# Expert rows gathered in four 256-column pieces and turned by VectorE block transposes; gate and up weights in contiguous rows; up in two halves

## The chip, the cores and the metric

The kernel runs on one core of one Trainium2 chip. The metric is the device time of one execution in microseconds (us), as the median of several runs; lower is better. Everything is float32. Five engines have a queue of their own each: TensorE (PE in the profile; PEld is its weight load), VectorE (DVE), ScalarE (ACT), GpSimd (POOL) and SyncE (SP). Each runs its instructions in the order in which they stand, and they meet at semaphores.

## The reference

One layer of an encoder, applied to a prompt of 2048 tokens and 8 x 16 sample tokens: 17 tiles of 128 tokens of width 1024. The change touches the query weights of the attention and the experts:

```python
def memory_attend(h, mem_k, mem_v, w_xq, w_xo):
    B, T, _ = h.shape
    q = (h @ w_xq).reshape(B, T, X_HEADS, X_HEAD_DIM)
    s = jnp.einsum('bqhd,bkhd->bhqk', q, mem_k.astype(q.dtype)).astype(jnp.float32) * (X_HEAD_DIM ** -0.5)
    p = jax.nn.softmax(s, axis=-1).astype(q.dtype)
    o = jnp.einsum('bhqk,bkhd->bqhd', p, mem_v.astype(q.dtype)).reshape(B, T, D_MODEL)
    return o @ w_xo

def routed_experts(t, expert, w_eg, w_eu, w_ed):
    # t: (n, 1024); expert: (n, 2), the two experts of 32 that each token takes; assignments sorted by expert
    ...
    def expert_block(args):
        xb, e = args
        return (jax.nn.silu(xb @ w_eg[e]) * (xb @ w_eu[e])) @ w_ed[e]
    ...

def trunk_layer(...):
    h = rms_norm(x, g_mix)
    z = h @ w_in
    ...
    x = x + jnp.concatenate([a_out, b_out], axis=-1) @ w_out
    x = x + memory_attend(rms_norm(x, g_xattn), mem_k, mem_v, w_xq, w_xo)
    x = x + hier_moe(rms_norm(x, g_ffn), w_rg, b_rg, w_re, b_re, w_eg, w_eu, w_ed)
    return x, new_hist, v
```

An expert has gate and up matrices of 1024 x 512 and a down matrix of 512 x 1024. `hier_moe` picks a group of 4, two experts of 8 in it, calls `routed_experts` and adds its two rows per token by their gates.

## The kernel before

The stages follow one another: mixing (17 tiles, to about 852 us), a fold of `w_xq` and `w_xo` into two matrices A and B, the sample attention, a stage of attention and router (17 tiles, to about 1530 us), and the expert stage (to the end).

**Token rows and their turn.** A product needs the features on the partitions. In the attention stage `turn_split` (L217) turns a tile of 128 x 1024 by one DVE block transpose; it leaves the features in another order than a PE transpose does, and `w_xq`, from which A is made, is loaded in four DMAs so as to match that order (L399).

**The experts.** The router stores for each expert a list of rows (token, place, gate) in `table_scratch`. An expert step works on 128 rows in two lanes of 64: lane 0 with one expert, lane 1 with another, each expert's weights in its part of W (a part holds gate, up and down, 4096 columns each). `both` (in PE's part) issues a pass for both lanes: 64 rows of lane 0 and 64 rows of lane 1 on the two halves of the array, each against 512 columns of its own expert. There are 42 steps: one for tile 0 that is mixed into the end of the attention stage, and 41 by `work`, called from `expert_steps` (L1416): three in a row, a loop of 12 passes over two steps, an inner loop of 5 passes over two steps, and four in a row.

**A step on PE** (`work`, L2176): gate in 8 calls of `both` into `psg`; up in 8 into `psu`; then the transposes of the next tile's rows (`turn_x`, into `pst`, 8) woven with those of the hidden rows (`turn_h`, 4); down in 16 passes into `psx`. ACT makes silu of the gate (L1746), copies the lower half of the turned hidden rows (L1751) and the lower half of the turned token rows (L1756). DVE multiplies silu by up in two halves (`hidden`, L1937), copies the upper halves (L1942, L1929), adds the result into the rows of the token (`add_x`, L1956) and scales the output (L1962, L1965). `hidden` waits for the whole of up.

**A step on POOL** (order of `work`, L1645): `gather_x` (L1580, the rows that the result is added to), `gather(t+2)` (L1572, the rows that go in, one indirect DMA of 128 rows of 4 KB), `fetch(t+3)` (L1556, two DMAs of 64 list rows, one per lane), `fetch_again(t+1)` (the same for the list that the scatter uses), `scatter_x` (L1586), a small power (L1593) and `scatter_out` (L1599). `gather_x` waits until the scatter of the tile before has landed. All of these transfers go through the software queue q0; the weights go through q1, issued by SP (`load_part`, L1274), which loads the next expert's gate, up or down matrix as soon as PE is done with the part that it replaces, in rows of 512 columns (2 KB) for gate and up and of 1024 columns (4 KB) for down.

**Between the router and the experts** the last router tile scatters its lists (L1551), then POOL fetches the lists of tile 1 and gathers its rows, PE turns them and the first step of the loop begins. The names in the traces are those of the memory: `r_pss` holds `psg` and `psu`, `r_psx` is `psx`, `r_psr` and `r_psk` are the two halves of the turned hidden rows, `r_x1n` the gathered rows, `r_h2T` the turned ones, `r_x1r` the hidden rows, `e_pair` and `e_spair` the two fetched lists.

## Time and profile before

| | us |
|---|---|
| median of 3 runs | 2493.62 (2493.59 to 2493.75) |
| profiled execution | 2493.03 |
| its span | 2491.4 |
| granted TensorE clock over the span | 0.991 |
| PE busy | 2421.9 (97%) |
| DVE busy | 942.2 (38%) |
| POOL busy | 559.3 (22%) |
| ACT busy | 470.4 (19%) |

A share of 97% says that PE is the engine to look at, but not whether a microsecond less of its work is a microsecond less of time: that is read from the waits of each stage. In the profile's 40 slices the DMA engines are the busiest in the expert stage, at 0.4 to 0.9 of the time, and nearly idle before it.

### The profile page before, as it was taken

Reading aid. Unit: us, or ns where it says so; the run is one execution under the profiler, and the core shown is the slowest. Engines: PE = TensorE matmul, PEld = TensorE weight load, DVE = VectorE, ACT = ScalarE, POOL = GpSimd, SP = SyncE. Lnnn points to the kernel's source line nnn. Section 1 sums busy time; section 2 is a strip of 40 time slices with the busy share of each in tenths; the row PEclk is TensorE's granted clock in tenths of the full one; section 3 lists DMA queues with packets and bytes.
Section 4 is the critical chain, followed back from the end, with each engine's and each line's share of the span. In section 5 each row is a group of like instructions: output and inputs, shape, how many; then the busy total and the mean of one; then the engine's idle time right before and its main releaser. Section 6 shows DMA issues by size and latency. Waiting matters only on the chain.

```text
span 2491.4 us, 29996 instructions
## 1 busy us (share of the span) xinstructions
PE 2421.9 (97%) x9375; PEld 1104.5 (44%) x9376; DVE 942.2 (38%) x2519; ACT 470.4 (19%) x1042; POOL 559.3 (22%) x711
## 2 busy tenths in 40 slices
PE   8999999999999997999999998999999999999998
PEld 4444444444444574455555553333333333333332
DVE  1586756747676102233333334122212222222222
ACT  2222222222111122222222221111111111111111
POOL 1122132222213100011111112232333322323231
PEclk9999999999999998999999999999999999999999
DMA  6211111011153516522222117967497749797994
GB/s 234 106 40 56 39 64 39 34 64 38 41 189 78 185 42 245 177 65 64 68 68 68 59 52 270 326 227 266 158 362 258 260 161 367 256 348 266 347 348 147
DMA packets 168279, 403.67 MB, mean 162 GB/s; under 512 B 25650, under 2 KB 34370, under 8 KB 168178
## 3 DMA queue, kind: packets, MB, share of 16 engines
q1 hardware_dynamic: 137314, 327.81, 37.9%
q0 software_dynamic: 30656, 74.14, 8.1%
q8 instruction: 51, 0.84, 0.1%
q10 hardware_dynamic: 216, 0.54, 0.1%
q14 instruction: 42, 0.34, 0.0%
HBM read 336.15 MB, written 80.66 MB: 167 GB/s over the span
## 4 chain that ended last, share of the span: by engine, by line
PE 58%; DMA 1%; issue 1%; DVE 0%; POOL 0%; ACT 0%; POOLq 0%; ACTq 0%; DVEq 0%
PE r_pss L2162 22%; PE r_psx L2162 11%; PE r_psx L2124 9%; PE r_pss L2105 9%; PE r_pst L2151 2%; PE r_psr L2133 1%; PE r_psr L2173 1%; PE r_pst L2116 1%; PE r_pss L2163 1%; PE r_pst L2097 1%; PE r_psk L2173 0%; PE r_psx L2163 0%; DMA table_scratch<-r_val,r_slot 0%; PE r_pss L2210 0%; DMA r_x1n<-h_scratch,e_token 0%
## 5 line engine op out<-in xcount | busy, mean ns | idle before, releaser
L2162 PE MATMUL r_pss<-W,r_h2T 128*64 x1312 | 572.3, 594 | 3.3 <-issue 3.3
L2163 PE MATMUL r_pss<-W,r_h2T 128*64 128x512 f32 x1312 | 572.4, 594 | 0.0
L788 PE MATMUL a_psz<-W 128*128 128x512 f32 x1088 | 479.4, 594 | 0.1
L626 DVE SCALAR_TENSOR_TENSOR yacc<-aext,pcol,yacc 128x256 f32<-128x256 f32 x928 | 370.8, 476 | 0.0
L2162 PEld LDWEIGHTS r_pss<-W,r_h2T 128*64 128x64 f32 x1312 | 180.1, 137 | 373.6 <-issue 373.6
L788 PEld LDWEIGHTS a_psz<-W 128*128 128x128 f32 x1088 | 203.0, 191 | 235.2 <-issue 234.7
L2162 PE MATMUL r_psx<-W,r_x1r 128*64 x656 | 290.1, 595 | 2.3 <-ACT r_x1r L1751 0.2
L2163 PE MATMUL r_psx<-W,r_x1r 128*64 128x512 f32 x656 | 290.3, 595 | 0.0
L2124 PE MATMUL r_psx<-W 128*128 128x512 f32 x544 | 236.5, 592 | 1.2 <-ACT W L1696 1.2
L2105 PE MATMUL r_pss<-W,r_h2T 128*128 128x512 f32 x512 | 224.4, 596 | 2.3 <-PEq L123 2.3
L2163 PEld LDWEIGHTS r_pss<-W,r_h2T 128*64 128x64 f32 x1312 | 180.2, 137 | 0.0
L491 POOL TENSOR_TENSOR W<-W 128x512 f32<-128x512 f32 x34 | 115.6, 3409 | 268.5 <-ACT W L603 268.5
L1937 DVE TENSOR_TENSOR r_x1r<-r_pss,r_x1r 128x256 f32<-128x256 f32 x84 | 31.7, 418 | 368.9 <-PE r_pss L2163 338.6
L2162 PEld LDWEIGHTS r_psx<-W,r_x1r 128*64 128x64 f32 x656 | 86.5, 137 | 172.8 <-issue 172.8
L2124 PEld LDWEIGHTS r_psx<-W 128*128 128x128 f32 x544 | 102.0, 190 | 123.4 <-issue 123.4
L2105 PEld LDWEIGHTS r_pss<-W,r_h2T 128*128 128x128 f32 x512 | 96.5, 191 | 117.9 <-issue 117.9
L1956 DVE SCALAR_TENSOR_TENSOR r_x<-r_psx,e_spair,r_x 128x512 f32<-128x512 f32 x84 | 63.0, 750 | 226.8 <-PE r_psx L2163 226.8
L955 PE MATMUL a_psz<-W,a_maT 128*128 128x512 f32 x272 | 122.3, 592 | 0.0
L955 PE MATMUL a_psz<-W 128*128 128x512 f32 x272 | 122.3, 592 | 0.0
L1586 POOL DMA_INDIRECT x_scratch<-r_x,e_stoken x41 | 42.6, 1039 | 343.6 <-DVE r_x L1956 322.7
L1776 ACT ACTIVATE r_x1r<-r_x 128x512 f32<-128x512 f32 x84 | 52.9, 630 | 288.6 <-DVE r_x L1956 288.5
L1551 POOL DMA_INDIRECT table_scratch<-r_val,r_slot x34 | 34.8, 1023 | 255.9 <-DVE r_slot L1909 250.8
(351 smaller groups left out, 2374.1 us busy)
## 6 DMA issues: line engine op xcount, KB each, us to landing
W<-in_w_expert_gate SPq DMA_DIRECT2D x32, 2048.0 KB, 11.6
W<-in_w_expert_up SPq DMA_DIRECT2D x32, 2048.0 KB
W<-in_w_expert_down SPq DMA_DIRECT2D x32, 2048.0 KB
W<-in_x_prompt SPq DMA_DIRECT2D x32, 512.0 KB, 4.2
...
```

Of the source, the lines that this page charges most:

```text
L491: pool.tensor_tensor(x, mixed[:, 512 * n:512 * n + 512], x, ALU.add).then_inc(S["x1_half"], 1)
L626: ins = dve.scalar_tensor_tensor(out=out, in0=src, scalar=w, in1=yacc[:, i, :], op0=ALU.mult, op1=ALU.add)
L788: last = pe.matmul(psz[bank][:], hT[t.par][:, k, :], w_in[bank][:, k, :], start=(k == 0), stop=(k == KD - 1))
L955: last = pe.matmul(psz[n][:], (maT[:, k, :] if k < CG else mbl[t.par][:, k - CG, :]), w_out[:, k, 512 * n:512 * n + 512], start=(k == 0), ...
L1586: pool.indirect_dma_start(out=x2_d.rearrange("t p d -> (t p) d"), out_offset=bass.IndirectOffsetOnAxis(ap=stoken[t.par][:], axis=0), in_=y ...
L1776: act.activation(junk_f, yb[t.par][:, 512 * m:512 * m + 512], ACT.Square, scale=1 / 32, accum_out=fss[:, t.par, m:m + 1]).then_inc(F["squa ...
L1956: dve.scalar_tensor_tensor(out=yb[t.par][:, c], in0=psx[:, c], scalar=spair[t.par][:, 1:2], in1=yb[t.par][:, c], op0=ALU.mult, op1=ALU.add ...
L2105: last = pe.matmul(pss[:, 2 * n:2 * n + 2, :].rearrange("p h n -> p (h n)"), h2T[i % 2][:, k, :], A[:, k, 512 * n:512 * n + 512], start=(k ...
L2124: last = pe.matmul(psx[:, 512 * n:512 * n + 512], (pT if i else qT)[:, c, :], (B if i else w_xo)[:, c, 512 * n:512 * n + 512], start=(c == ...
L2151: last = pe.transpose(pst[:, k, :], xg[t.par][:, P * k:P * k + P], ident[:])
L2162: pe.matmul(out[0:HALF, :], xt[:, 0:HALF], W[:, bass.ds(base + at, 512)], start=start, stop=stop)
L2163: return pe.matmul(out[HALF:P, :], xt[:, HALF:P], W[:, at:at + 512], start=start, stop=stop)
```

## The change

1. `turn_split` reads its source at a stride of 8 elements, which gives the feature order 8p + k on partition p. `w_xq` is loaded in that order in one DMA, and the norm's gains (`gx`) by a small DMA of its own.
2. Gate and up matrices are loaded as 8 consecutive rows per partition (16 KB in one piece). Down is as before.
3. The rows of an expert tile are gathered by four indirect DMAs of 128 x 256 columns (1 KB per row), each with its own column of indices 4 x token + quad. The index columns come from four fetches of 128 x 3 in place of two of 64 x 3. One DVE `turn_split` turns the tile; PE's `turn_x` and the copies on ACT and DVE are gone, also for tile 0, whose transposes stood in the scores of the last token tile.
4. Up is computed in two halves of 256 columns, the first into `psu`, the second into `psk`, and `hidden` half 0 waits for the first only. Both halves of the hidden rows are turned right behind up.

```diff
         def turn_split(dve, dst, src):
 
-            return dve.transpose(dst.rearrange("p k (b r) -> p b k r", r=QUAD), src.rearrange("p (b k a) -> p b k a", b=QUADS, a=QUAD))
+            return dve.transpose(dst.rearrange("p k (b r) -> p b k r", r=QUAD), src.rearrange("p (b a k) -> p b k a", b=QUADS, a=QUAD))
...
-                            for q in range(QUADS):
-                                sp.dma_start(w_xq[QUAD * q:QUAD * q + QUAD, :, :],
-                                             I["w_xq"][0][D // QUADS * q:D // QUADS * q + D // QUADS, :].rearrange("(k a) n -> a k n", a=QUAD)).then_inc(wxq_here, 16)
+                            sp.dma_start(w_xq, I["w_xq"][0].rearrange("(p k) n -> p k n", p=P)).then_inc(wxq_here, 16)
...
+                    act.dma_start(gx[:], I["g_xattn"][0].rearrange("(p k) -> p k", p=P)).then_inc(gx_here, 16)
...
-                                                  scale=gcol[:, KD + k:KD + k + 1])
+                                                  scale=gx[:, k:k + 1])
...
-                          I[name][0][bass.ds(e, 1), :, :].rearrange("a (k p) n -> p (a k) n", p=P)).then_inc(here, 16)
+                          I[name][0][bass.ds(e, 1), :, :].rearrange("a (k p) n -> p (a k) n" if n == 2 else "a (p k) n -> p (a k) n", p=P)).then_inc(here, 16)
...
-            psh = [psr[:].rearrange("p (j n) -> p j n", j=4), psp]
+            psh = psr[:].rearrange("p (j n) -> p j n", j=4)
+            psh_hi = psu[:, 256:512].rearrange("p (j n) -> p j n", j=2)
+            ups = [psu[:, 0:256], psk[:, 0:256]]
...
+                    def fetch_quad(par, lane, h, rows):
+
+                        pool.dma_start(pair[par][:, 2 * lane + h, :], rows.unsqueeze(0).to_broadcast([QUADS, QUAD, 3])).then_inc(pair_here[par], 16)
+
                     def fetch(t):
                         need(pool, T["token_done"], t.v - 1)
                         settle(pool)
-                        fetch_pairs(t, pair[t.par], pair_here[t.par])
+                        for lane in range(LANES):
+                            base = pool.value_load(steps_row[0:1, lane, bass.ds(t.v, 1)], min_val=0, max_val=NE * REG - HALF)
+                            for h in range(2):
+                                fetch_quad(t.par, lane, h, table_d[bass.ds(base + QUAD * h, QUAD), :])
 
                     def fetch_again(t):
...
                     def gather(t):
                         pool.wait_ge(T["token_done"], t.v + 1)
-                        need(pool, T["x_turned"], 2 * (t.v - 1))
+                        need(pool, T["xT_done"], t.v - 1)
                         settle(pool)
-                        pool.indirect_dma_start(out=xg[t.par][:], out_offset=None,
-                                                in_=h3_d[0:P * (EARLY + 2), :] if isinstance(t.v, int) and t.v == 0 else h3_d,
-                                                in_offset=bass.IndirectOffsetOnAxis(ap=token[t.par][:], axis=0)).then_inc(x_here[t.par], 16)
+                        h3_rows = h3_d[0:P * (EARLY + 2), :] if isinstance(t.v, int) and t.v == 0 else h3_d
+                        for b in range(QUADS):
+                            c = D // QUADS
+                            pool.indirect_dma_start(out=xg[t.par][:, c * b:c * b + c], out_offset=None,
+                                                    in_=h3_rows.rearrange("t (q c) -> (t q) c", q=QUADS),
+                                                    in_offset=bass.IndirectOffsetOnAxis(ap=token[t.par][:, b:b + 1], axis=0)).then_inc(x_here[t.par], 16)
...
                     def tokens(t):
-                        dve.wait_ge(pair_here[t.par], 32 * (t.half + 1))
-                        need(dve, x_here[t.par], 16 * t.half)
-                        dve.tensor_copy(token[t.par][:], pair[t.par][:, 0:1]).then_inc(T["token_done"], 1)
+                        dve.wait_ge(pair_here[t.par], 16 * QUADS * (t.half + 1))
+                        need(dve, x_here[t.par], 16 * QUADS * t.half)
+                        dve.tensor_scalar(token[t.par][:], pair[t.par][:, :, 0], float(QUADS), quad[:], ALU.mult, ALU.add).then_inc(T["token_done"], 1)
 
                     def xT_out(t):
-                        dve.wait_ge(T["x_turned"], 2 * t.v + 2)
+                        dve.wait_ge(x_here[t.par], 16 * QUADS * (t.half + 1))
                         need(dve, T["up_done"], t.v)
-                        dve.tensor_copy(xT[t.par][:, 4:8, :], pst[:, 4:8, :]).then_inc(T["xT_done"], 1)
+                        turn_split(dve, xT[t.par][:], xg[t.par][:]).then_inc(T["xT_done"], 1)
 
                     def hidden(t):
                         dve.wait_ge(T["silu_done"], t.v + 1)
-                        dve.wait_ge(T["up_done"], t.v + 2)
                         need(dve, T["h_turned"], 2 * t.v)
                         for m in range(2):
+                            if m == 0 and not (isinstance(t.v, int) and t.v == 0):
+                                dve.wait_ge(T["up_half"], t.v)
+                            else:
+                                dve.wait_ge(T["up_done"], t.v + 2)
                             c = slice(256 * m, 256 * m + 256)
-                            dve.tensor_tensor(hb[:, c], psu[:, c], sg[:, c], ALU.mult).then_inc(T["h_done"], 1)
+                            up = psu[:, c] if isinstance(t.v, int) and t.v == 0 else ups[m]
+                            dve.tensor_tensor(hb[:, c], up, sg[:, c], ALU.mult).then_inc(T["h_done"], 1)
 
                     def hT_out(t):
                         dve.wait_ge(T["h_turned"], 2 * t.v + 2)
                         dve.wait_ge(T["down_done"], t.v + 1)
-                        dve.tensor_copy(hT[:, 2:4, :], psh[1][:, 0:2, :]).then_inc(T["hT_hi"], 1)
+                        dve.tensor_copy(hT[:, 2:4, :], psh_hi).then_inc(T["hT_hi"], 1)
...
-                    def turn_x(t, ks):
-                        if ks[0] == 0:
-                            pe.wait_ge(x_here[t.par], 16 * (t.half + 1))
-                            need(pe, T["xT_done"], 2 * t.v)
-                        for k in ks:
-                            last = pe.transpose(pst[:, k, :], xg[t.par][:, P * k:P * k + P], ident[:])
-                        if ks[-1] in (3, 7):
-                            last.then_inc(T["x_turned"], 1)
-
                     def weights(t):
                         e = pe.value_load(steps_row[0:1, 2, bass.ds(t.v, 1)], min_val=0, max_val=EPL - 1)
                         wanted = pe.value_load(steps_row[0:1, 3, bass.ds(t.v, 1)], min_val=16, max_val=16 * NE)
                         return pe.value_load(slot_base[0:1, bass.ds(e, 1)], min_val=EXPERT_COLS, max_val=2 * EXPERT_COLS), wanted
 
-                    def both(out, xt, base, at, start, stop):
-
-                        pe.matmul(out[0:HALF, :], xt[:, 0:HALF], W[:, bass.ds(base + at, 512)], start=start, stop=stop)
-                        return pe.matmul(out[HALF:P, :], xt[:, HALF:P], W[:, at:at + 512], start=start, stop=stop)
+                    def both(out, xt, base, at, start, stop, n=512):
+
+                        pe.matmul(out[0:HALF, :], xt[:, 0:HALF], W[:, bass.ds(base + at, n)], start=start, stop=stop)
+                        return pe.matmul(out[HALF:P, :], xt[:, HALF:P], W[:, at:at + n], start=start, stop=stop)
 
                     def turn_h(t, m):
                         pe.wait_ge(T["h_done"], 2 * t.v + m + 1)
-                        if m and isinstance(t.v, int) and t.v == 1:
-                            pe.wait_ge(T["loads_known"], 1)
                         if m == 0:
                             need(pe, T["hT_lo"], t.v)
                             need(pe, T["hT_hi"], t.v)
                         for k in (2 * m, 2 * m + 1):
-                            last = pe.transpose(psh[m][:, k - 2 * m, :], hb[:, P * k:P * k + P], ident[:])
+                            last = pe.transpose(psh_hi[:, k - 2, :] if m else psh[:, k, :], hb[:, P * k:P * k + P], ident[:])
                         last.then_inc(T["h_turned"], 1)
 
                     def work(t, j=-LAST):
                         base, wanted = second if isinstance(t.v, int) and t.v == 1 else weights(t)
                         pe.wait_ge(gate_here, wanted)
-                        pe.wait_ge(T["xT_done"], 2 * t.v + 2)
+                        pe.wait_ge(T["xT_done"], t.v + 1)
                         need(pe, T["silu_done"], t.v)
                         for k in range(KD):
                             last = both(psg, xT[t.par][:, k, :], base, 512 * k, k == 0, k == KD - 1)
                         last.then_inc(T["gate_done"], 1)
                         pe.wait_ge(up_here, wanted)
                         need(pe, T["h_done"], 2 * t.v)
-                        for k in range(KD):
-                            last = both(psu, xT[t.par][:, k, :], base, 4096 + 512 * k, k == 0, k == KD - 1)
-                        last.then_inc(T["up_done"], 1)
-                        more = j < LAST - 1
-                        if more:
-                            turn_x(t.at(1), (0, 1, 2, 3))
+                        for m in range(2):
+                            if m and isinstance(t.v, int) and t.v == 1:
+                                pe.wait_ge(T["loads_known"], 1)
+                            for k in range(KD):
+                                last = both(ups[m], xT[t.par][:, k, :], base, 4096 + 512 * k + 256 * m, k == 0, k == KD - 1, 256)
+                            last.then_inc(T["up_done" if m else "up_half"], 1)
                         turn_h(t, 0)
-                        if more:
-                            turn_x(t.at(1), (4, 5))
                         turn_h(t, 1)
-                        if more:
-                            turn_x(t.at(1), (6, 7))
                         pe.wait_ge(down_here, wanted)
...
                             scores(s, 0)
-                            if s + 1 == NT:
-                                pe.wait_ge(S["pT_done"], NT - 2)
-                                turn_x(fixed(0), (0, 1, 2, 3))
-                                turn_x(fixed(0), (4, 5, 6, 7))
                             scores(s, 1)
...
-                    turn_x(fixed(1), (0, 1, 2, 3))
-                    turn_x(fixed(1), (4, 5, 6, 7))
```

In the body of the first expert loop on PE, between the end of up and the first down pass, stood before (`r_pst` the turned token rows):

```order
L2163 MATMUL r_pss<-W,r_h2T 64x512
L2148 ISA
L88 ISA
L2151 MATMUL r_pst<-ident,r_x1n 128x128 x4
L2166 REGISTER_ALU
L2173 MATMUL r_psr<-ident,r_x1r 128x128 x2
L2151 MATMUL r_pst<-ident,r_x1n 128x128 x2
L2173 MATMUL r_psk<-ident,r_x1r 128x128 x2
L2151 MATMUL r_pst<-ident,r_x1n 128x128 x2
L2162 ISA
L2162 MATMUL r_psx<-W,r_x1r 64x512
```

and stands now, with two 256-column passes of up's second half ahead:

```order
L2161 MATMUL r_psk<-W,r_h2T 64x256
L2162 MATMUL r_psk<-W,r_h2T 64x256
L2161 ISA
L2161 MATMUL r_psk<-W,r_h2T 64x256
L2162 MATMUL r_psk<-W,r_h2T 64x256
L2165 REGISTER_ALU
L2170 MATMUL r_psr<-ident,r_x1r 128x128 x2
L2165 REGISTER_ALU
L2170 MATMUL r_pss<-ident,r_x1r 128x128 x2
L2161 ISA
L2161 MATMUL r_psx<-W,r_x1r 64x512
```

The eight token transposes have gone, and the two pairs of hidden transposes follow each other directly.

On POOL, in the body of the loop, from `gather_x` to `scatter_x` before:

```order
L1580 DMA r_x<-x_scratch,e_stoken 128x1024
L1569 REGISTER_ALU
L88 REGISTER_ALU
L1572 DMA r_x1n<-h_scratch,e_token 128x1024
L88 REGISTER_ALU
L1555 ISA
L1555 TENSOR_LOAD p_steps_row
L1555 ISA x2
L1556 ISA
L1556 DMA e_pair<-table_scratch 64x3
L1555 ISA
L1555 TENSOR_LOAD p_steps_row
```

and now:

```order
L1596 DMA r_x<-x_scratch,e_stoken 128x1024
L1582 REGISTER_ALU
L1588 DMA r_x1n<-h_scratch,e_token 128x256 x4
L88 REGISTER_ALU
L1572 ISA
L1572 TENSOR_LOAD p_steps_row
L1572 ISA x2
L1566 ISA
L1566 DMA e_pair<-table_scratch 128x1x3
L1566 ISA
L1566 DMA e_pair<-table_scratch 128x1x3
L1572 ISA
```

Four gathers stand in the place of one, and two fetches follow each reading of the step's numbers; the fetches of `e_spair` and the scatter follow as before.

## Rows read from the trace of the kernel before

**Rows 1.** The page, costliest groups: line, names, count, busy us, mean ns, idle before

```profile
L2162 PE MATMUL r_pss<-W,r_h2T 128*64 x1312 | 572.3, 594 | 3.3 <-issue 3.3
```

**Rows 2.** Windows: length, busy us of PE, PEld, DVE, ACT, POOL, clock, DMA, GB/s

```profile
1610.00:2380.00 770.00, 767.61 (x3696) 284.44 (x3692) 169.51 (x376) 99.46 (x240) 233.96 (x309) 1.00 0.77 276
```

**Rows 3.** Timeline of a step, PE then DVE: start us, us, engine, instruction

```profile
1814.06 0.59 PE L2162 MATMUL r_pss<-W,r_h2T 128*64 x1
...
1814.48 0.59 PE L2162 MATMUL r_pss<-W,r_h2T 128*64 x1
...
1815.71 0.44 PE L2173 MATMUL r_psr<-ident,r_x1r 128*128 128x128 f32 x2
...
1816.42 0.38 PE L2151 MATMUL r_pst<-ident,r_x1n 128*128 128x128 f32 x2
1816.89 0.64 PE L2162 MATMUL r_psx<-W,r_x1r 128*64 x1
...
1815.23 0.75 DVE L1937 TENSOR_TENSOR r_x1r<-r_pss,r_x1r 128x256 f32<-128x256 f32 x2 [9.07 <-PE r_pss L2163]
```

**Rows 4.** Timeline of the last step, PE then DVE

```profile
2470.54 0.59 PE L2162 MATMUL r_pss<-W,r_h2T 128*64 x1
...
2472.66 0.64 PE L2162 MATMUL r_psx<-W,r_x1r 128*64 x1 [0.23 <-ACT r_x1r L1751]
...
2471.19 0.75 DVE L1937 TENSOR_TENSOR r_x1r<-r_pss,r_x1r 128x256 f32<-128x256 f32 x2 [8.64 <-PE r_pss L2163]
```

**Rows 5.** Timeline of PE in the sample stage, passes of 256 columns

```profile
951.79 0.38 PE L1238 MATMUL s_pss<-W,s_only 128*32 128x256 f32 x1
...
952.00 0.38 PE L1238 MATMUL s_pss<-W,s_only 128*32 128x256 f32 x1
...
952.87 0.38 PE L1238 MATMUL s_pss<-W,s_only 128*32 128x256 f32 x1
```

**Rows 6.** Timeline of POOL over one step

```profile
1802.99 1.05 POOL L1586 DMA_INDIRECT x_scratch<-r_x,e_stoken  x1 [11.63 <-DVE r_x L1956]
...
1812.42 0.99 POOL L1580 DMA_INDIRECT r_x<-x_scratch,e_stoken  x1 [4.34 <-DMA x_scratch<-r_x,e_stoken]
1813.71 0.96 POOL L1572 DMA_INDIRECT r_x1n<-h_scratch,e_token  x1 [0.30 <-issue]
1814.68 0.61 POOL L1556 DMA_DIRECT2D e_pair<-table_scratch  x1
...
1818.23 0.52 POOL L1556 DMA_DIRECT2D e_spair<-table_scratch  x1 [0.72 <-issue]
1825.61 1.04 POOL L1586 DMA_INDIRECT x_scratch<-r_x,e_stoken  x1 [6.87 <-DVE r_x L1956]
```

**Rows 7.** Line L1580 on POOL, what its idle time waited for: us, times

```profile
  DMA x_scratch<-r_x,e_stoken: 102.6, 25
```

**Rows 8.** DMA queues in 1817 to 1820.3 us: packets, MB, share of 16 engines

```profile
q0 software_dynamic: 226, 0.86, 66.9%
q1 hardware_dynamic: 227, 0.46, 36.6%
```

**Rows 9.** The transition: the chain of waits, then the timelines of POOL and DVE

```profile
1537.78 4.20 DMA e_pair<-table_scratch
...
1543.32 4.49 DMA r_x1n<-h_scratch,e_token
...
1547.85 1.97 PE r_pst L2151 x8
...
1550.80 1.11 PE r_pss L2162
...
1545.59 0.52 POOL L1556 DMA_DIRECT2D e_pair<-table_scratch  x1 [0.63 <-issue]
...
1548.22 0.15 DVE L1924 CAST e_token<-e_pair 128x1 int32<-128x1 f32 x1 [4.57 <-DMA e_pair<-table_scratch]
```

**Rows 10.** Line L219, the block transposes of the attention stage: ns min/median/max

```profile
L219 DVE STREAM_TRANSPOSE r_h2T<-r_x1n x16: 1236/1237/1245, 970.8 to 1433.2; 128x1024 f32<-128x1024 f32 x16
```

**Rows 11.** The chain of waits at the end of the attention stage

```profile
1467.38 0.87 PE r_pst L2151 x8
```

**Rows 12.** The chain of waits where PE leaves the second loop

```profile
2387.35 2.32 issue
```

62 lines of the change are left out of this document (29 added, 33 removed).

## The prediction

> **What bounds the kernel now.** I read the page first. Its line groups show TensorE (PE) busy 97% of the span, and its costliest group is the expert product of one lane, 1312 instructions: 41 steps of 32 [rows 1]. A step is one pair of half tiles, 48 passes of 512 columns (gate 16, up 16, down 16) with a few transposes between. Over 770 us of the expert stage PE is busy for 767.6 us, and the 16 DMA engines 77% of the time [rows 2]: PE waits for nobody there, so a step is the sum of what PE issues. A pass follows the one before after 0.42 to 0.43 us (1814.06, 1814.48), so 48 take 20.6 us.
>
> The rest is the gap between the last up pass and the first down pass. It is 1816.89 - 1814.48 = 2.41 us, 1.98 beyond the pass itself [rows 3]. In it VectorE (DVE) multiplies both halves of `hidden` (0.75), PE turns the two halves of the hidden rows, and eight transposes of the next step's token rows are woven between, the last two at 1816.42. The last step has no such token transposes and shows what is left without them: from 2470.54 to 2472.66, 1.69 us beyond the pass [rows 4].
>
> **Up in two halves.** Sixteen passes of 512 columns become 32 of 256. The nearest row of a 256-column pass is a column-tiled one in the sample stage: 0.21 us from 951.79 to 952.00 [rows 5], 0.216 on average up to 952.87. 32 x 0.216 = 6.91 against 16 x 0.429 = 6.86: +0.05 us a step.
>
> **The gap.** With half 0 of `hidden` done during the second half of up, and the token transposes gone from PE, what follows the start t of the last pass is: the record of a 256-column pass is 0.38 long where one of 512 is 0.59 [rows 3, 5], and DVE began 0.16 after the record's end (1815.23 against 1814.48 + 0.59), so it begins at t + 0.54. Two overlapped halves took 0.75, so one takes about 0.42 and ends at t + 0.96. The transposes follow at t + 1.0, the second 0.11 later, and the first down pass 0.36 after the second (1816.42 + 0.11 to 1816.89). That is t + 1.4 to 1.5, or 1.2 us beyond the pass of 0.216. Bounds: 0.93, if DVE ends 0.3 earlier, as a shorter pass may let it, and 1.69, the last step's row, if nothing of it shrinks. A step saves 1.98 - 1.2 - 0.05 = 0.73 us, between 0.24 and 1.0. I take 0.73, since its pieces are this place's own rows. 40 steps: -29.2 us (-10 to -40). The last step gains 1.69 - 1.2 - 0.05 = -0.4.
>
> **Transposes of the first tile's rows.** They leave the score products of the last token tile, where eight took 0.87 us on the path [rows 11]: -0.9.
>
> **Turns on DVE.** One block transpose of 128x1024 takes 1.24 us from a contiguous order [rows 10]. The new one reads at a stride of 32 bytes, which no row shows: I bound it by 1.24 and, my own choice, twice that, and take 1.24 for the sum. In a step DVE is idle for over three quarters (169.5 us busy of 770 [rows 2]). The turn stands after the copy of the hidden rows, beside 6.9 us of down passes, and only the next gate pass needs it: nothing. What it delays on its own engine is `add_x`, by up to 1.2 us more than the copy that it replaces, and `add_x` leads to `scatter_x` (below).
>
> The Trainium skill has a rule that speaks against this edit: "SBUF — State Buffer", section "Door 1: The DMA port swizzle", says that each access that crosses to a new line of 16 bytes pays a penalty. No row of this trace shows it and the page gives no size; by it I would take the upper bound, hidden in a step, and the sum would be 1 us later at the transition.
>
> **Gather and fetch on GpSimd (POOL).** In a step POOL issues scatter_x at S = 1802.99, gather_x at S + 9.4, gather at S + 10.7, then four fetches, the last from 1818.23 to S + 15.8; it is idle until the next scatter_x at 1825.61 [rows 6]. The spare time is 6.9 us in 22.6. An indirect DMA costs 1.29 from issue to issue (1812.42 to 1813.71), a plain one about 1.2. Three more gathers cost 3.9. Two more fetches cost 1.2, since they read no new numbers of the step (0.61 each), or up to 2.6 if a list of 128 rows costs like an indirect one. That is 5.1 to 6.5 us, and POOL ends at S + 20.9 to S + 22.3, where a step is to last 22.57 - 0.73 = 21.85. But a wait is in it: gather_x waited in 25 of 41 steps for the scatter to land (102.6 us in all, 4.1 each [rows 7]), and without it starts at about S + 5.3. So the mean is at most (25 x 22.3 + 16 x 18.1) / 41 = 20.7, below 21.85, and a late scatter has most of a step ahead of it, since its rows are needed by the next `add_x` only. I cost it at nothing, with a rival for the opposite.
>
> **Weight rows of 16 KB.** Gate and up come as 16 KB per partition in place of eight pieces of 2 KB. While both queues have work they alternate packet by packet: 226 packets of the software queue beside 227 of the hardware queue in 3.3 us, the latter 36.6% of 16 engines, that is 85 ns each, the former 156 ns [rows 8]. At the same rate 16 KB hold a DMA engine for 8 x 85 = 0.68 us. The loads themselves take no longer, and PE waited for none of them [rows 2], so they gain nothing either. But a gather, a scatter or a fetch that shares an engine with them waits 0.6 us longer at each of its packets, at 8 packets an engine 4.8 us. That goes to POOL's chain alone, and to the rival on it.
>
> **The transition** from router to experts has no cover. The chain of waits goes: last fetch issued at 1537.78, landed 4.2 us later; gather issued at 1543.32, landed 4.49 later; eight transposes, copies, gate at 1550.80 [rows 9]. Now there are four fetches of the token column in place of two (1.2 to 2.4 us), then four gathers (3 x 1.29 = 3.9). The transposes and copies (2.95 from 1547.85 to 1550.80) give way to one turn of 1.24 to 2.5. DVE, however, runs `tokens(2)` ahead of that turn, which waits for the fetch behind the gathers: it was issued at 1545.59 and served DVE at 1548.22, 2.63 later [rows 9]. With gathers to 1549.2 and four fetches at 1.15 each the last is issued at about 1553.8, lands at 1556.4, the turn ends at 1557.8 and gate starts near 1558.2: +7 us (+5 to +10).
>
> **At nothing:** w_xq comes as one transfer in place of four, asked for in the last iterations of mixing and used only by the fold after them; the small load of the gain column goes ahead of the rest on ACT's queue, under the first x tiles; counts, waits and tile shapes cost no instruction on PE. `both` for 32 passes has 16 more register instructions a step on PE's sequencer, hidden in passes that run meanwhile.
>
> **The sum:** 2493.6 - 29.2 - 0.4 - 0.9 + 7 = 2470.1. It is made against the profiled execution (2493.03, span 2491.4), which is 0.6 below the median; the difference carries over to 2493.62.
>
> **Rivals.**
> B, *the gap hardly shrinks*: down still waits for copies through the same three engines as in the last step (1.69 [rows 4]), and the transition costs the upper 9: 2493.6 - 10 - 0.9 + 9 = 2491.7. For it: that row has no token transposes and is yet 1.69. Against: it still has both halves of `hidden` in it, one of which goes.
>
> C, *slower, by the chain of scatters*. Scatter_x(t) must land before gather_x(t+1) and POOL issues all between. If its packets meet those of 16 KB, the 25 contended steps take 22.3 + 4.8 = 27.1 us, against 18.1 in the other 16: a mean of 23.6, above 21.85. It decides once the mean passes the step, since the slack of one step is used up once: 41 x (23.6 - 21.85) = +72, so about 2542. The same holds if `tokens(t+2)`, at the head of DVE's step, waits for a fetch that lies behind such gathers: `hidden` and `down` stand behind it. For it: DMA engines are 77% busy and POOL's spare 6.9 us are spent. Against: the scatter starts as down ends, when only gate weights can be under way.
>
> D, *PE's loop outgrows what stays fetched*. The loop body of two steps grows from 514 to 626 instructions. Where PE entered other code it stood for 2.32 us (at 2387.35, "issue" [rows 12]). If each of 17 passes of the loops paid that: +39, 2470 + 39 = 2509. Against it: 770 us of the loop show 2.4 us without work in all [rows 2]. The Trainium skill's page "Runtime: NRT & Kernel Launch", section "Instruction fetch mechanics", says that only two blocks of 256 instructions are held and that a branch outside them fetches anew; by it the body of 514 would already have stalled, which the row denies. The same section grants PE a store of 2048 instructions, which agrees.
>
> **Chances.** Forecast 0.76 (2455 to 2484), B 0.08, C 0.11, D 0.05. The range of 8 in 10 goes from 2455 (saving 1.0 a step) to 2492 (B). A measurement tells about 0.2% (5 us) from no change: faster 0.76, same 0.08, slower 0.16.
>
> **What would show it.** Gap from the last 256-column pass to the first down pass 1.3 to 1.5 us, with DVE's half 0 of `hidden` inside the second half of up; passes at 0.216; gate of step 1 near 1557; PE idle in no step; POOL's scatter_x to scatter_x about 21.9. Wrong if PE waits for `added` or the turned rows in steps (C), if 2.3 us of "issue" come once per loop pass (D), or if the gap stays at 1.7 (B).

## The result, and the profile after

| | before | after |
|---|---|---|
| time, median (lowest to highest), us | 2493.05 (2488.81 to 2494.36) | 2496.32 (2492.11 to 2502.0) |
| profiled execution / its span, us | 2493.03 / 2491.4 | 2495.43 / 2493.8 |

The ratio is 1.0018, with an interval of 1.001 to 1.0027: 3 us slower, where 2470 was forecast and the range ended at 2492. Both medians are over 14 executions.

The page of the changed kernel shows less work on PE and more on DVE and POOL than before, as the change meant. Its first lines, and the groups of the gather and of the fetch (line engine op, names, count, busy us, mean ns, idle before):

```profile
span 2493.8 us, 32514 instructions
PE 2392.3 (96%) x10351; PEld 1162.8 (47%) x10352; DVE 1019.0 (41%) x2522; ACT 452.1 (18%) x1001; POOL 753.1 (30%) x921
L1588 POOL DMA_INDIRECT r_x1n<-h_scratch,e_token x168 | 161.0, 958 | 56.7 <-issue 53.6
L1566 POOL DMA_DIRECT2D e_pair<-table_scratch x168 | 118.1, 715 | 6.0 <-issue 5.9
```

The stretch of [rows 2], as windows (busy us of PE, PEld, DVE, ACT, POOL; clock, DMA share, GB/s), the largest wait of PE in 1600 to 2380 us, and a wait of DVE in 1555 to 2480 (idle us in all, most of it there in an undisturbed step too; times; longest):

```profile
1610.00:2380.00 770.00, 745.81 (x4542) 336.08 (x4540) 221.96 (x378) 82.65 (x205) 389.99 (x477) 1.00 0.78 277
PE r_pss L2170 <- DVE r_x1r L1948: 13.8, 25, 3.0
DVE r_x1r L1948 <- remote: 102.0, 16, 9.4
```

PE is busy for 745.8 us of the 770 where it was busy for 767.6: a step now has less work for PE, but PE also stands still for 24 us. PE's wait is at the transposes of the hidden rows, for DVE's product, and 16 times DVE's start of that product has a releaser that the profile doesn't know ("remote"). No such row stands in e1, e3, f3 or f4 below. An undisturbed step shows the change doing what it says. PE, then DVE, then ACT, in step 2:

```profile
1594.08 0.38 PE L2161 MATMUL r_psk<-W,r_h2T 128*64 x1
...
1594.39 0.44 PE L2170 MATMUL r_psr<-ident,r_x1r 128*128 128x128 f32 x2
1594.99 0.44 PE L2170 MATMUL r_pss<-ident,r_x1r 128*128 128x128 f32 x2 [0.16 <-DVE r_x1r L1948]
1595.50 0.64 PE L2161 MATMUL r_psx<-W,r_x1r 128*64 x1
...
1591.15 0.43 DVE L1948 TENSOR_TENSOR r_x1r<-r_pss,r_x1r 128x256 f32<-128x256 f32 x1 [5.58 <-PE r_pss L2162]
1594.51 0.42 DVE L1948 TENSOR_TENSOR r_x1r<-r_psk,r_x1r 128x256 f32<-128x256 f32 x1 [2.93 <-PE r_psk L2162]
...
1594.87 0.38 ACT L1768 ACTIVATE r_x1r<-r_psr 128x256 f32<-128x256 f32 x1 [6.67 <-PE r_psr L2170]
```

The gap is 1595.50 - 1594.08 = 1.42 us, where [rows 3] had 2.41, and half 0 of `hidden` lies inside the second half of up. DVE begins half 1 0.43 after the start of the last pass. Now step 13, with PE, DVE, ACT and POOL:

```profile
1840.83 0.38 PE L2161 MATMUL r_psk<-W,r_h2T 128*64 x1
...
1841.15 0.44 PE L2170 MATMUL r_psr<-ident,r_x1r 128*128 128x128 f32 x2
1843.54 0.44 PE L2170 MATMUL r_pss<-ident,r_x1r 128*128 128x128 f32 x2 [1.95 <-DVE r_x1r L1948]
1843.90 0.64 PE L2161 MATMUL r_psx<-W,r_x1r 128*64 x1
...
1843.06 0.43 DVE L1948 TENSOR_TENSOR r_x1r<-r_psk,r_x1r 128x256 f32<-128x256 f32 x1 [4.75 <-remote]
...
1843.10 0.38 ACT L1768 ACTIVATE r_x1r<-r_psr 128x256 f32<-128x256 f32 x1 [8.06 <-PE r_psr L2170]
...
1835.78 1.01 POOL L1596 DMA_INDIRECT r_x<-x_scratch,e_stoken  x1 [0.64 <-issue]
1837.10 0.98 POOL L1588 DMA_INDIRECT r_x1n<-h_scratch,e_token  x1 [0.30 <-issue]
...
1840.90 0.95 POOL L1588 DMA_INDIRECT r_x1n<-h_scratch,e_token  x1 [0.30 <-issue]
```

The last up pass has the same form, and nothing else is queued on DVE, but DVE starts 2.23 us after it instead of 0.43: 1.8 late. ACT, which waits for PE's first transposes (1841.15), starts 1.95 us after them instead of 0.48: 1.5 late. The trace also records the time of each signal (semaphore update) itself, and these are late by the same 1.8 and 1.5. So it is PE's word that it is done which is late, not the engines that wait for it. PE's next instructions are recorded on time meanwhile, but the ends of its passes are modelled, so the trace doesn't tell whether the array itself was behind. Meanwhile POOL issues gather_x and the four gathers. In step 2 they began 6.7 us after the first up pass, behind most of the stage; here they begin 3.0 us after it and fall among its 32 short passes.

Going through all 41 steps of this trace, the signal for half 0 came late in 11 (up to 3.8 us) and the one for the end of up in 12 (up to 2.8). In all of these steps the gathers start 1.6 to 5.7 us after the first up pass, and in no step in which they start later is a signal of up late. The gate's 512-column passes had no late signal, and down, under which the burst falls in most steps, had one (the last of step 37, 1.0 us, while DVE was waiting for a transfer anyway). PE itself paused too: near the end of up in six steps (6, 7, 10, 11, 17 and 21), for 0.3 to 1.0 us each. All six are among those with a late signal of half 0. In step 6 a pass came 0.92 us after the one before in place of 0.22, while DVE got the word of a pass of 1678.28 only at 1682.55:

```profile
1681.52 0.38 PE L2161 MATMUL r_psk<-W,r_h2T 128*64 x1
1682.44 0.38 PE L2161 MATMUL r_psk<-W,r_h2T 128*64 x1 [0.54 <-issue]
...
1682.55 0.42 DVE L1948 TENSOR_TENSOR r_x1r<-r_pss,r_x1r 128x256 f32<-128x256 f32 x1 [9.34 <-remote]
```

A long pause has a second price. After the gap of 4.12 us in step 36 the down passes follow each other at 0.85 us, not 0.43, and the windows row shows the granted clock at 0.50 (1.2 GHz, against 2.4 in the row above):

```profile
2358.41 1.12 PE L2161 MATMUL r_psx<-W,r_x1r 128*64 x1
2359.32 1.06 PE L2161 MATMUL r_psx<-W,r_x1r 128*64 x1
2358.30:2361.70 3.40, 3.40 (x10) 1.00 (x10) 2.37 (x2) 0.00 (x0) 2.09 (x4) 0.50 0.90 130
```

That cost 1.6 us. The gate of step 38 took 1.7 us more at the lower clock too, but that is no part of the late signals' cost: it follows the pause of 2.3 us where PE leaves the second loop, and `f4_fetch_early` and `e6_rows_8k` below, which have no late signals, pay it as well. The kernel before has the same pause, with a granted clock of 1.00 behind it.

### The profile page after: what moved, and what is told of

Same layout as the page of the kernel before. It is cut to its first block, busy times and chain, and to the rows that moved or that the text cites. A ratio compares the mean times of both kernels' runs of the same rounds, so it can differ in the third digit from the quotient of the medians.

```text
span 2493.8 us, 32514 instructions
## 1 busy us (share of the span) xinstructions
PE 2392.3 (96%) x10351; PEld 1162.8 (47%) x10352; DVE 1019.0 (41%) x2522; ACT 452.1 (18%) x1001; POOL 753.1 (30%) x921
## 4 chain that ended last, share of the span: by engine, by line
PE 56%; another core or an unknown queue 2%; issue 1%; DVE 1%; ACT 0%; POOL 0%; DVEq 0%; ACTq 0%; POOLq 0%
PE r_pss L2161 16%; PE r_psx L2161 11%; PE r_psx L2132 9%; PE r_pss L2115 9%; PE r_psk L2161 5%; PE r_psr L2141 1%; PE r_pss L2170 1%; DVE r_x1r L1948 1%; PE r_pst L2124 1%; PE r_pst L2107 1%; PE r_pss L2162 1%; PE r_psk L2162 0%; PE r_pss L2203 0%; PE r_psx L2241 0%
## 5 line engine op out<-in xcount | busy, mean ns | idle before, releaser
L2161 PE MATMUL r_pss<-W,r_h2T 128*64 x1312 | 434.1, 489 | 16.2 <-issue 16.2
L2162 PE MATMUL r_pss<-W,r_h2T 128*64 128x256 f32 (+1 forms) x1312 | 434.1, 489 | 0.0
L1588 POOL DMA_INDIRECT r_x1n<-h_scratch,e_token x168 | 161.0, 958 | 56.7 <-issue 53.6
L2162 PE MATMUL r_psk<-W,r_h2T 128*64 128x256 f32 x656 | 149.5, 379 | 1.0 <-issue 1.0
L2161 PE MATMUL r_psk<-W,r_h2T 128*64 x656 | 148.6, 379 | 1.1 <-issue 1.1
L1566 POOL DMA_DIRECT2D e_pair<-table_scratch x168 | 118.1, 715 | 6.0 <-issue 5.9
```

The lines of the kernel that those rows point to most:

```text
L1566: pool.dma_start(pair[par][:, 2 * lane + h, :], rows.unsqueeze(0).to_broadcast([QUADS, QUAD, 3])).then_inc(pair_here[par], 16)
L1588: pool.indirect_dma_start(out=xg[t.par][:, c * b:c * b + c], out_offset=None, in_=h3_rows.rearrange("t (q c) -> (t q) c", q=QUADS), in_off ...
L2161: pe.matmul(out[0:HALF, :], xt[:, 0:HALF], W[:, bass.ds(base + at, n)], start=start, stop=stop)
L2162: return pe.matmul(out[HALF:P, :], xt[:, HALF:P], W[:, at:at + n], start=start, stop=stop)
```

## The experiments

Below, the **expert stage** is the time from the first gate pass of step 1 to the first down pass of the last step, read from each trace. It leaves out the stages ahead, which wobble by some 4 us from run to run (the mixing stage ended at 850.0 us before, 850.3 after, 846.7 in `e3_rows_2k`). A **session** is one set of kernels run one after the other on one chip, with the kernel before among them. "Late" means late signals from PE as above. e3, e7, f5, g1 and g2 pair features with the wrong weight rows: the work is the same, the result is not.

| kernel | session | gathers | gate/up rows | up | median us | ratio [interval] | expert stage | late |
|---|---|---|---|---|---|---|---|---|
| before | - | 1 | 2 KB | whole | 2493.05 | 1 | 921.9 | no |
| after | - | 4 in up | 16 KB | halves | 2496.32 | 1.0018 [1.001, 1.0027] | 920.4 | yes |
| e1 | 1 | 4 in up | 16 KB | whole | 2493.01 | 1.0007 [0.9998, 1.0016] | 922.2 | no |
| e2 | 1 | 4 behind up | 16 KB | halves | 2473.85 | 0.9918 [0.9904, 0.9933] | 899.4 | no |
| e3 | 1 | 4 in up | 2 KB | halves | 2473.34 | 0.9928 [0.9914, 0.9942] | 898.8 | no |
| e4 | 1 | 1, PE turns | 2 KB | halves | 2484.0 | 0.9969 [0.9959, 0.998] | 914.6 | no |
| e5 | 2 | 4 in up | 2 KB | halves | 2472.33 | 0.9928 [0.9911, 0.9944] | 899.2 | no |
| e6 | 2 | 4 in up | 8 KB | halves | 2469.35 | 0.9919 [0.9903, 0.9936] | 898.9 | no |
| e7 | 2 | 1, PE turns | 16 KB | halves | 2485.47 | 0.9972 [0.9961, 0.9984] | 915.9 | no |
| e8 | 2 | 4 behind up | 2 KB | halves | 2472.8 | 0.9926 [0.9909, 0.9942] | 899.9 | no |
| f2 | 3 | 4 in up | 16 KB | halves, one signal | 2530.72 | 1.0166 [1.014, 1.0192] | 956.9 | yes |
| f3 | 3 | 4 in up | 16 KB | whole, two signals | 2495.04 | 1.0018 [1.0008, 1.0027] | 922.0 | 4 x 0.35 |
| f4 | 3 | 4 behind up | 16 KB | halves | 2472.11 | 0.9936 [0.9913, 0.9959] | 898.9 | no |
| f5 | 3 | 4 in up, PE turns | 16 KB | halves | 2518.58 | 1.0118 [1.0096, 1.014] | 949.6 | yes |
| g1 | 4 | 4 in up | 16 / 2 KB | halves | 2523.34 | 1.0133 [1.0102, 1.0163] | 952.0 | yes |
| g2 | 4 | 4 in up | 2 / 16 KB | halves | 2513.09 | 1.0084 [1.0056, 1.0111] | 939.6 | yes |
| g4 | 4 | 2 in up, 2 behind | 16 KB | halves | 2473.37 | 0.9935 [0.9918, 0.9952] | 899.1 | half 0 only |
| g6 | 4 | 4 in up, PE turns | 2 KB | halves | 2583.13 | 1.0367 [1.0348, 1.0386] | 1010.8 | yes, worst |
| h1 | 5 | 4 in up | 16 KB | halves | 2499.04 | 1.0025 [1.0012, 1.0037] | 923.5 | yes |
| h2 | 5 | 4 in up | 8 KB | halves | 2504.05 | 1.0053 [1.0037, 1.0069] | 927.2 | yes |

The kernel before stood at medians of 2492.86, 2491.29, 2490.72, 2489.63 and 2491.51 us in sessions 1 to 5. Whether a kernel lags belongs to the session and not to the single execution: all ten executions of h1 and six of h2 took over 2490 us, all four of e6 under 2475.

### Session 1: each part undone

Two theories stand against each other in the expectations. In P the issue of POOL's indirect DMAs while short passes run holds up PE's signals; in W it is the 16 KB rows, or the gathers' own chain.

`e1_up_whole`, up whole again:

```diff
-                            for k in range(KD):
-                                last = both(ups[m], xT[t.par][:, k, :], base, 4096 + 512 * k + 256 * m, k == 0, k == KD - 1, 256)
-                            last.then_inc(T["up_done" if m else "up_half"], 1)
+                        for k in range(KD):
+                            last = both(psu, xT[t.par][:, k, :], base, 4096 + 512 * k, k == 0, k == KD - 1)
+                        last.then_inc(T["up_done"], 1)
```

> The changed kernel with up in 16 passes of 512 columns again; hidden half 0 waits for all of up. Theory P (what holds TensorE back is the issue of GpSimd's indirect DMAs while passes of 256 columns run): with passes of 512 columns no semaphore of TensorE comes late, every step has the same gap of about 1.7 us beyond the last pass (that of the last step before the change), a step takes 22.3 us, and the time is 2493 - 40 x 0.3 + 4 at the transition = about 2485 us. Theory W (the 16 KB packets of the weights, or the gathers' chain, hold TensorE back): the late steps stay, and the time is that of the changed kernel or more, 2495 to 2505 us.

`e2_gather_late`, the four gathers not before up is done:

```diff
+                            pool.wait_ge(T["up_done"], t.v + 2)
+                            settle(pool)
                             gather(t.at(2))
```

> The changed kernel, but GpSimd waits for the end of up before it issues the four gathers (one wait added), so that they fall into the gap and the down passes of 512 columns. Theory P: no semaphore of TensorE late by more than 0.2 us, gaps of 1.42 to 1.5 us in nearly all 41 steps, time about 2472 us. Theory W: the late steps stay, time 2493 us or more. If the gathers' own chain is what is late (theory G), the later gathers make it worse: over 2500 us.

`e3_rows_2k`, gate and up in pieces of 2 KB as before:

```diff
-...rearrange("a (k p) n -> p (a k) n" if n == 2 else "a (p k) n -> p (a k) n", p=P)
+...rearrange("a (k p) n -> p (a k) n", p=P)
```

> The changed kernel with gate and up weights in 2 KB rows in the old order (the products then pair features with the wrong weight rows; the work is the same). Theory P: same late steps, 2494 to 2498 us. Theory W: the late steps go, about 2472 us.

`e4_halves_only`, the kernel before with up in halves and nothing else:

> The kernel before with up in two halves alone: TensorE transposes, one gather, 2 KB rows as before. Hidden half 0 is ready early, so the gap falls from 1.98 to about 1.8 us beyond the pass. Theory P: in the 16 steps in which GpSimd issues its two indirect DMAs during up there is some lag of TensorE's semaphores, shorter than in the changed kernel (under 1.5 us), since two are issued and not five; time 2486 to 2496 us. Theory W: no lag at all, every step 22.3 to 22.4 us, 2485 us.

None of the four had late signals. e1 and e2 came out so by theory P, though e1's time was forecast as 2485 and was 2493.01; e3 went against P and for W; e4 fitted W. So every part that was undone seemed to be needed. One result held up in all that followed: neither part of the step's change is worth much alone. e1, in which the token transposes are gone but up is whole, has steps of 22.45 to 22.53 us against 22.45 and 22.62 before: 0.04 us gained. PE in one of its steps:

```profile
1930.63 0.59 PE L2159 MATMUL r_pss<-W,r_h2T 128*64 x1
...
1931.76 0.44 PE L2168 MATMUL r_psr<-ident,r_x1r 128*128 128x128 f32 x2 [0.52 <-DVE r_x1r L1946]
...
1932.89 0.64 PE L2159 MATMUL r_psx<-W,r_x1r 128*64 x1 [0.37 <-ACT r_x1r L1768]
```

PE waits where it used to transpose. e4, with halves but the token transposes still woven in, has steps of 22.34 and 22.42: 0.16 gained. Both together give 21.90 and 21.98, 0.60 gained. Each had been hidden behind the other.

I took e3's 2473.34 for proof that the 16 KB rows were the cause, and built session 2 on it. But no kernel in session 1 showed the late signals, so nothing shows that any would have.

### Session 2: row size

`e5_rows_2k_right` has 2 KB rows with gate and up interleaved, so that the numbers are right again; `e6_rows_8k` has pieces of 8 KB; `e7_halves_16k` is e4 with 16 KB rows; `e8_2k_late` is e5 with e2's wait.

```diff
+                eng.dma_start(dst.rearrange("p (g c) -> p g c", g=2)[:, :, 2048 * n:2048 * n + 2048],
+                              src.rearrange("a (p g r) n -> p (a g) (r n)", p=P, g=2)).then_inc(here, 16)
```

(the load of `e6_rows_8k`)

> The changed kernel with the right rows, but gate and up of an expert interleaved in W (gate row, up row, ...), so that a load lands in 8 pieces of 2 KB per partition again; all gathers stay in the up phase. Theory R (it takes rows of 16 KB together with four gathers during passes of 256 columns): no semaphore of TensorE late, about 2472 us, as with the wrong rows. Theory D (the rows' contents or something else of e3 made the difference): late steps as in the changed kernel, 2495 us.

> The same with pieces of 8 KB. If the lag grows with the length of a piece: some late steps, 2475 to 2490 us. If it has a threshold above 8 KB: none, 2472 us. If anything above 2 KB is enough: 2495 us.

> Up in halves alone (kernel before plus that), with gate and up weights in 16 KB rows (the products pair features with the wrong weight rows; the work is the same). If one gather of 4 KB rows during up is enough for the lag: late steps, over 2490 us. If it takes the burst of four gathers: 2484 us as with 2 KB rows, no late semaphore.

> Both remedies together: pieces of 2 KB and the gathers behind the end of up. Either alone takes all the lag away, so together they bring nothing more: 2472 us, with equal steps of 21.9 us.

No kernel of session 2 had late signals. e5, e6 and e8 agree within 3.5 us; e7 shows that 16 KB rows without the burst of gathers cost nothing in a session without late signals (915.9 against e4's 914.6; the difference is 1.7 us of lower clock in step 38). It all fitted the row theory, but no kernel of the session had both 16 KB rows and the burst.

### Session 3: which ingredient

`f2_no_mid_semaphore` gives up the signal of half 0, `f3_whole_mid_semaphore` adds one to whole passes, `f5_halves_16k_burst` is e7 with its gather in four pieces, and `f4_fetch_early` moves the gathers behind the fetches and behind up:

```diff
-                        if j < LAST - 2:
-                            gather(t.at(2))
...
+                        if j < LAST - 2:
+                            pool.wait_ge(T["up_done"], t.v + 2)
+                            settle(pool)
+                            gather(t.at(2))
```

(`f4_fetch_early`), and

```diff
-                            last.then_inc(T["up_done" if m else "up_half"], 1)
+                            if m:
+                                last.then_inc(T["up_done"], 1)
```

(`f2_no_mid_semaphore`; DVE's half 0 waits for `up_done`)

> The changed kernel, still 32 passes of 256 columns, 16 KB rows and four gathers during up, but no semaphore after the first half: hidden half 0 waits for all of up. If the passes of 256 columns are what falls behind (theory Q): the semaphore at the end of up is late in some ten or more steps, 2510 us or more, since the gap is longer by a half of hidden too. If only a semaphore that falls due in the middle is held up (theory M): no late semaphore at the end of up, steps of 22.3 us, about 2487 us.

> The changed kernel with up in 16 passes of 512 columns, plus a semaphore (that nobody waits for) on the last pass of k = 3, in the middle of up. Theory Q: it is on time in all steps, 2493 us as without it. Theory M: it comes 2 to 4 us late in the steps in which the gathers start early in up, as up_half does in the changed kernel.

> The changed kernel with GpSimd's fetches first, in the up phase, and the four gathers behind the end of up. If the burst of gathers is one of the causes: no late semaphore, 2472 us, as with both moved. If it was the broadcast fetches, which the other experiment moved too: late semaphores of 1 to 3 us again, 2485 to 2495 us.

> The kernel before plus up in halves, 16 KB rows (the products pair features with the wrong weight rows) and the gather in four pieces of 1 KB rows; transposes on TensorE and fetches as before. If these three together are enough: late semaphores in the 16 or so steps in which the gathers start early in up, 2495 to 2505 us. If the DVE turn or the fetches are needed as well: none, 2485 us as with one gather.

f2 is slower by 1.7%: it is not the number of signals that does it. One signal fewer leaves the one that remains on the path, and it was late in 9 steps, by up to 2.6 us. Its last up pass of one step, and DVE behind it:

```profile
2131.07 0.38 PE L2159 MATMUL r_psk<-W,r_h2T 128*64 x1
...
2134.12 0.42 DVE L1946 TENSOR_TENSOR r_x1r<-r_pss,r_x1r 128x256 f32<-128x256 f32 x1 [10.01 <-remote]
```

f3 has the burst, the 16 KB rows and the middle signal, but 512-column passes: the middle signal was never late, the last one by 0.35 us in 4 steps. f5 keeps PE's transposes and the old fetches and lags heavily, at 2518.58. So DVE's turn and the new fetches are not needed for it. That e7, with one gather, had 2485.47 doesn't show that the four pieces made the difference: e7 ran in session 2, in which nothing lagged. f4 is clean in the session in which f2 and f5 lag. POOL of one of its steps, and DVE's two halves:

```profile
1741.94 0.99 POOL L1596 DMA_INDIRECT r_x<-x_scratch,e_stoken  x1 [4.87 <-DMA x_scratch<-r_x,e_stoken]
1743.16 1.49 POOL L1566 DMA_DIRECT2D e_pair<-table_scratch  x2 [0.23 <-issue]
...
1749.24 1.04 POOL L1588 DMA_INDIRECT r_x1n<-h_scratch,e_token  x1 [0.37 <-issue]
...
1740.91 0.42 DVE L1951 TENSOR_TENSOR r_x1r<-r_pss,r_x1r 128x256 f32<-128x256 f32 x1 [5.61 <-PE r_pss L2165]
1744.30 0.42 DVE L1951 TENSOR_TENSOR r_x1r<-r_psk,r_x1r 128x256 f32<-128x256 f32 x1 [2.96 <-PE r_psk L2165]
```

The fetches fall into up and the gathers into down; its steps last 21.90 and 21.98 in turn, and no signal of PE's is late in any of them.

### Session 4: row size once more, and the size of the burst

`g1_gate_16k` and `g2_up_16k` are the changed kernel with 16 KB rows for one of the two matrices; `g6_halves_2k_burst` is f5 with 2 KB rows; `g4_two_late` splits the burst:

```diff
-                            gather(t.at(2))
+                            gather(t.at(2), (0, 1))
+                            pool.wait_ge(T["up_done"], t.v + 2)
+                            settle(pool)
+                            gather(t.at(2), (2, 3))
```

> The changed kernel with only gate's rows in 16 KB, up's in 2 KB (the up product pairs features with the wrong weight rows; the work is the same). If lag grows with the share of long transfers: fewer late steps, 2480 to 2490 us. If only those that are issued just ahead of the up phase matter: the steps after a gate load are late (7, 11, 17, 22, 28, 34) and those without a load (6, 10, 20, 21) are not.

> The changed kernel with only up's rows in 16 KB, gate's in 2 KB (the gate product pairs features with the wrong weight rows). By the same two readings: fewer late steps in all, or late ones only where an up load runs during up, that is steps 12 and 36 and no others; 2473 to 2490 us.

> The changed kernel with two of the four gathers in their place and two behind the end of up. If the lag grows with the number of gathers in the up phase: late semaphores of 1 to 2 us, 2475 to 2485 us. If it takes more than three indirect DMAs in a row: none, 2472 us.

> The kernel before plus up in halves and the gather in four pieces, with 2 KB weight rows as before: the run with 16 KB rows less the rows alone. If long rows are one of three causes: no late semaphore, all steps 22.3 to 22.4 us, 2485 us. If the earlier absence of late steps had to do with wrong numbers or another layout of W: late steps as with 16 KB rows, 2510 us or more.

The row theory fell. g6 has 2 KB rows for gate and up and is the slowest of all, 2583.13. g1 and g2 missed both of their forecasts (2523.34 and 2513.09, and late too in steps 6, 10, 20 and 21, which have no load). g6's windows row shows PE busy for 716 us of 770, and the clock at 0.98:

```profile
1610.00:2380.00 770.00, 716.17 (x4338) 335.07 (x4336) 161.51 (x428) 90.35 (x217) 300.79 (x372) 0.98 0.69 243
```

g4 shows that gather_x and two gathers among the short passes suffice to delay the signal of half 0 (in 11 steps, by up to 2.1 us). But that signal has 3 us of slack, and the end of up, with POOL issuing nothing by then, was on time: 899.1 for the stage. In f5, g1, g2 and g6 PE itself paused within up as well, in 10 to 12 steps and for 13 to 20 us in all.

### Session 5: the free kernel again

`h1_changed_again` is the changed kernel and `h2_rows_8k_again` is e6, neither with any edit.

> The changed kernel itself, once more, beside the next one on one chip. The runs with late semaphores and those without them came from different chips, so the chip may be what the row length seemed to be. Theory C (some chips fall behind, whatever the rows): either both of this pair lag or neither, 2495 us or more or 2472 us. Theory R (rows of 16 KB): this one lags, 2495 us.

> Pieces of 8 KB, four gathers during up, once more. Theory C: late semaphores if and only if the changed kernel has them on this chip, 2495 us or more or 2470 us. Theory R: none on any chip, 2470 us.

h2 took 2504.05 us where the same program had taken 2469.35 in session 2, while the kernel before kept its time (2491.51 and 2491.29). Here are the two in the same step: half 0 on DVE, its last pass on PE, gather_x on POOL, and the stretch of [rows 2] as windows; h2 first:

```profile
1683.57 0.42 DVE L1953 TENSOR_TENSOR r_x1r<-r_pss,r_x1r 128x256 f32<-128x256 f32 x1 [9.28 <-remote]
...
1679.36 0.38 PE L2166 MATMUL r_pss<-W,r_h2T 128*64 x1
...
1676.38 0.99 POOL L1601 DMA_INDIRECT r_x<-x_scratch,e_stoken  x1 [0.31 <-issue]
...
1610.00:2380.00 770.00, 741.69 (x4484) 332.61 (x4482) 220.96 (x371) 82.52 (x204) 388.27 (x476) 1.00 0.78 273
```

```profile
1672.39 0.42 DVE L1953 TENSOR_TENSOR r_x1r<-r_pss,r_x1r 128x256 f32<-128x256 f32 x1 [5.57 <-PE r_pss L2167]
...
1671.89 0.38 PE L2166 MATMUL r_pss<-W,r_h2T 128*64 x1
...
1668.91 1.00 POOL L1601 DMA_INDIRECT r_x<-x_scratch,e_stoken  x1 [0.31 <-issue]
...
1610.00:2380.00 770.00, 758.33 (x4604) 342.96 (x4606) 228.65 (x385) 84.94 (x210) 402.39 (x493) 1.00 0.80 285
```

From gather_x to half 0 it is 7.19 us in the one and 3.48 in the other. PE's passes stand alike against POOL in both: the last pass of half 0 starts 2.98 us after gather_x (1679.36 and 1671.89). So the same work in the same position draws the delay in one session and not in the other. Sessions 2 and 5 ran on different chips; whether it is the chip or something else of a session was not separated. Sessions 1 and 5 bear the same chip number, but no kernel ran in both.

**What is settled:** the delay comes where 256-column passes and a burst of indirect DMAs from POOL fall together. In the sessions that show it, f3 (long passes) and f4 (only gather_x and the fetches under the short passes) are free of it but for f3's 0.35 us, and g4 (gather_x and two gathers) has it at half 0 alone, where it costs nothing. In the changed kernel's own trace the late signals of up stand only in steps where the burst falls into up, and nearly the same steps are late in h1 (DVE's product with "remote" in the same six steps up to 1860 us in both). f5 shows that it doesn't matter who turns the rows, and g6 that 2 KB rows don't prevent it. Nor did more bytes move through the queue. This is q0 in the stretch of [rows 2], before and after (packets, MB, share of 16 engines):

```profile
q0 software_dynamic: 23936, 60.07, 21.1%
q0 software_dynamic: 27829, 60.66, 23.4%
```

Nor is it the fetching of PE's code: the queue of instructions (q8) moves no packet from 1665 to 2176 us of the changed kernel, and twelve of the late steps lie there.

e1, e2, e3, e5, e6 and e8 come from sessions in which nothing lagged; they can't tell a remedy from luck, and of the row size they say nothing.

**What stays open:** by what path POOL's burst reaches PE, and why it depends on the session. Nothing in the traces separates a delay of the signals alone from one of the array: in most late steps the passes are recorded at 0.216 us while the signals lag, yet PE pauses in six steps of the changed kernel and in a dozen of g6. Three runs were not made. None has halves and the single old gather (two indirect DMAs under up, with gather_x) in a session that lags, so the number at which the delay begins lies between f4's one and g4's three. None has short passes in another number than 32, so f3 changes their length and their number together. And none issues the four gathers in another order or from another queue.

## Why the prediction was wrong

**The step that failed** is "Gather and fetch on GpSimd (POOL)", and in it "I cost it at nothing". The working looked only at whether POOL's own chain fits into a step, and it does: POOL's spare time sufficed, as DVE waited only 7 times for gather_x's landing (35.9 us in all) and PE never did. What it left out is where the burst stands against PE's passes. In the changed kernel the expert stage is 920.4 us, in kernels with the same steps and no late signals 898.9 (e6, f4): the late signals cost 21.5 us. Step by step against e6, 15.4 of it lie in longer gaps, 4.3 in PE's pauses within up, 1.6 in the lower clock of step 36 and 0.2 in the gate of step 1. Against 921.9 before, e6 and f4 show 23.0 saved: 24.7 by the steps, less 1.7 for the lower clock in step 38. The term was not merely mis-sized, since the wait that it left out is another one than the chain that it looked at; no row of the trace before could show it, since there a burst met 512-column passes only and the 256-column ones of [rows 5] met no burst.

**Rival C**, the slower one, had the right place, indirect DMAs on POOL, and the wrong mechanism: no chain of scatters set the pace, and 2542 was far off. That its direction came true is luck. **Rival B** fell (gap 1.42, not 1.9). **Rival D** fell: f4 has such a pause of "issue" on PE once, where PE leaves the second loop, as in [rows 12]. The windows row behind it has the lower clock of step 38:

```profile
2368.91 0.64 PE L2164 MATMUL r_pss<-W,r_h2T 128*64 x1 [2.31 <-issue]
...
2369.60:2373.00 3.40, 3.40 (x10) 1.02 (x8) 1.06 (x2) 0.56 (x2) 2.18 (x3) 0.50 1.03 390
```

Term by term, in us:

| term | predicted | measured |
|---|---|---|
| pass of 256 columns | 0.216 | 0.216 (15 passes, 1590.84 to 1594.08) |
| gap beyond the pass | 1.2 | 1.20 and 1.28 in turn |
| saved in a step | 0.73 | 0.60 |
| saved in the last step | 0.4 | 0.65 |
| transposes of the first tile | -0.9 | -0.9 |
| transition | +7 (+5 to +10) | +4.3 |
| turn on DVE | 1.24 (bound 2.5), hidden | 2.03, hidden |
| 16 KB rows | nothing | nothing seen (e7 against e4: 1.3 us in a stage of 915, from the clock in step 38) |
| lower clock in step 38 | not seen | +1.7 |
| late signals | not seen | +21.5 |

The forecast saving of a step was too large because steps come in pairs with gaps of 2.24 and 2.41 us, and I had read the longer. From the start of the attention stage to the first gate pass it took 559.36 us before and 562.79 after, +3.4. The stage's last score pass of the last tile comes 0.9 earlier for the first-tile transposes that have gone, which leaves +4.3 for the transition. The gathers there ended 1.7 us earlier than forecast (the fetches behind them begin at 1547.50, not 1549.2), and the four fetches cost less than the 1.15 each that I had given them:

```profile
1547.50 2.78 POOL L1566 DMA_DIRECT2D e_pair<-table_scratch  x4
```

That is 0.70 each. In the loop, where each pair of fetches follows a reading of the step's numbers, it is 0.70 as well. Those 3.5 us less, and 0.8 more for DVE's turn, make the difference from 7. (The gate of step 1 began at 1554.60; my sum had 1558.2 for it and my list of signs, wrongly, 1557.) DVE's turn did reach the upper part of its bounds. All turns, with min, median and max in ns:

```profile
L221 DVE STREAM_TRANSPOSE r_h2T<-r_x1n x58: 1998/2030/2042, 971.1 to 2453.5; 128x1024 f32<-128x1024 f32 x58
```

A stride of 32 bytes costs 1.64 times the contiguous 1237 ns of [rows 10]. By the penalty for crossing to a new 16-byte line in the Trainium skill ("SBUF — State Buffer", "Door 1: The DMA port swizzle"), the trace agrees in direction, and gives the size that the page doesn't.

With the measured terms and no late signal the sum would have been 2493.6 - 23.0 + 3.4 = 2474.0. From the 2490.72 of f4's session the same terms give 2471.1, and f4 took 2472.11. That is no independent test, since the 23.0 is read from f4 and e6 themselves; it says that nothing outside these two stretches moved by more than about 1 us.

**The better version** is f4: 0.9936 [0.9913, 0.9959] in a session in which its siblings lagged, below the kernel before and the changed one. g4, at 0.9935, is as fast. e6's 0.9919 is no better a choice, since the same program took 1.0053 in session 5.
